# A layout edit: constants, dump and statistics move between activations and weight buffers, and two side chunks swap buffers

## What is computed

```
for i in range(DEPTH):                       # DEPTH = 2
    hn = rms_norm(h, gains[0])
    mix = retention(hn, ...) if i % 2 == 0 else gated_deltanet(hn, ...)
    h = h + rms_norm(mix, gains[1])
    ff = sq_relu_mlp(rms_norm(h, gains[2]), mlp_w_up[i], mlp_w_down[i])
    h = h + rms_norm(ff, gains[3])
```

## The kernel before

| | before |
|---|---|
| resid | 0 |
| act_hi, act_lo | 16, 32 |
| w_raw, w_hi, w_lo | 48, 64, 80 |
| gains | 96 |
| square (constants), dump, stat | 104, 105.5, 107.5 |
| big_at | 107.6875 |
| side_hi0 to 3; also hid_hi, y_hi, go_hi from the first | 107.6875 + 0, 8, 16, 24 |
| side_lo0 to 3; also hid_lo, y_lo, go_lo from the first | 107.6875 + 32, 40, 48, 56 |
| normed, raw_side, mix | 107.6875 + 64, 80, 80 |

## Time and profile before

### The profile page before, as it was taken

How to read it: one execution, slowest core, us unless ns; L and a number is a source line. 1 busy time by engine, 2 the same in 40 slices (tenths; PEclk the granted TensorE clock), 3 DMA queues, 4 the chain that set the end, 5 groups by cost and what they waited for, 6 DMA issues and landing times.

```text
span 1476.7 us, 19863 instructions
## 1 busy us (share of the span) xinstructions
PE 1448.8 (98%) x7772; PEld 1216.7 (82%) x7772; DVE 596.1 (40%) x1096; ACT 544.2 (37%) x1037; POOL 650.7 (44%) x303
## 2 busy tenths in 40 slices
PE   8999999999999999999999999999998999999998
PEld 7988888657889888888888977889988988888886
DVE  5551002363264420044037445797756640024224
ACT  5232233254253222223235457754734322123231
POOL 5244344443544443444546216357435444444442
PEclk9999999999999999999999999999999999999999
DMA  6222323400333223223232222221113132232321
GB/s 245 103 86 91 109 85 111 145 1 29 101 102 115 86 86 113 86 85 114 86 114 90 86 87 89 83 86 40 49 58 129 58 107 93 89 110 86 107 93 57
DMA packets 66557, 136.23 MB, mean 92 GB/s; under 512 B 3632, under 2 KB 4016, under 8 KB 66096
## 3 DMA queue, kind: packets, MB, share of 16 engines
q1 hardware_dynamic: 64016, 125.90, 25.9%
q10 hardware_dynamic: 2464, 9.25, 1.7%
HBM read 133.03 MB, written 2.11 MB: 92 GB/s over the span
## 4 chain that ended last, share of the span: by engine, by line
PE 89%; DVE 4%; ACT 2%; POOL 2%; DMA 1%; issue 1%; SPq 0%; DVEq 0%; ACTq 0%
PE bank L457 27%; PE bank L458 27%; PE bank L459 27%; PE bank L668 2%; POOL side_lo L332 1%; PE bank L782 1%; PE bank L654 1%; PE bank L738 1%; DVE mix L1614 1%; DMA w_raw<-in_ret_w_in_dram 1%; DVE gv L1846 1%; PE bank L505 1%; DVE act_lo L1656 0%; PE bank L686 0%; DVE resid L1612 0%
## 5 line engine op out<-in xcount | busy, mean ns | idle before, releaser
L332 POOL TENSOR_TENSOR w_lo<-w_raw,w_hi 128x1024 fp32r<-128x1024 f32 (+1 forms) x216 | 515.5, 2409 | 687.3 <-ACT w_hi L1058 675.5
L1058 ACT ACTIVATE w_hi<-w_raw 128x1024 fp32r<-128x1024 f32 x208 | 208.9, 1054 | 467.1 <-PE bank L459 424.5
L457 PE MATMUL bank<-act_hi,w_hi 128*128 128x512 f32 (+1 forms) x816 | 294.7, 361 | 6.6 <-DVE act_lo L1656 4.4
L459 PE MATMUL bank<-act_hi,w_lo 128*128 128x512 f32 (+1 forms) x816 | 293.0, 359 | 0.0
L458 PE MATMUL bank<-act_lo,w_hi 128*128 128x512 f32 (+1 forms) x816 | 292.9, 359 | 0.0
L458 PE MATMUL bank<-w_lo,hid_hi 128*128 128x512 f32 x480 | 189.0, 394 | 0.0
L457 PE MATMUL bank<-w_hi,hid_hi 128*128 128x512 f32 x480 | 188.3, 392 | 0.0
L459 PE MATMUL bank<-w_hi,hid_lo 128*128 128x512 f32 x480 | 186.5, 388 | 0.0
L1768 DVE TENSOR_TENSOR relu_sq<-relu 128x512 f32<-128x512 f32 x64 | 48.6, 759 | 328.6 <-ACT relu L1084 328.0
L457 PEld LDWEIGHTS bank<-act_hi,w_hi 128*128 128x128 f32 x816 | 154.7, 190 | 31.5 <-DVE act_lo L1656 5.5
L459 PEld LDWEIGHTS bank<-act_hi,w_lo 128*128 128x128 f32 x816 | 154.6, 189 | 22.7
(11 more groups left out here) (282 smaller groups left out, 2167.5 us busy)
## 6 DMA issues: line engine op xcount, KB each, us to landing
w_raw<-in_mlp_w_up_dram SPq DMA_DIRECT2D x32, 1024.0 KB, 5.7
w_raw<-in_mlp_w_down_dram SPq DMA_DIRECT2D x32, 1024.0 KB, 5.0
w_raw<-in_ret_w_in_dram SPq DMA_DIRECT2D x22, 1024.0 KB, 5.0
w_raw<-in_gdn_w_in_dram SPq DMA_DIRECT2D x16, 1024.0 KB, 5.4
w_raw<-in_ret_w_out_dram SPq DMA_DIRECT2D x8, 1024.0 KB, 4.9
w_raw<-in_gdn_w_out_dram SPq DMA_DIRECT2D x4, 1024.0 KB, 5.0
gains<-in_norm_gains_dram ACTq DMA_DIRECT2D x7, 512.0 KB, 6.2
raw_side<-in_ret_w_in_dram SPq DMA_DIRECT2D x2, 1024.0 KB, 15.0
```

The source lines that it names most:

```text
L332: done = nc.gpsimd.tensor_tensor(LO[slot][:, kt, :], RAW[raw][:, kt, :], HI[slot][:, kt, :].bitcast(F32), ALU.subtract)
L457: pe.matmul(dst, sta_hi, mov_hi, start=first, stop=False)
L459: return pe.matmul(dst, sta_lo, mov_hi, start=False, stop=last)
L1058: act.activation(HI[raw if slot is None else slot][:, kt, :], RAW[raw][:, kt, :], ACT.Copy)\
```

## The change

`square`, `dump` and `stat` (1536 + 2048 + 192 = 3776 bytes) are placed ahead of `w_raw` instead of behind `gains`. `w_raw`, `w_hi`, `w_lo` and `gains` thus lie 3.6875 KB higher: at 51.6875, 67.6875, 83.6875 and 99.6875; `square` is at 48. `resid`, `act_hi`, `act_lo` and everything from `big_at` on stay. In borders 0 and 3 chunk 2 takes slot 5 and chunk 3 slot 4, where it was the other way round. Nothing else differs.

```
@@ -85,16 +85,16 @@
     act_lo = plan.tile("act_lo", [P, KT, T], F32R, act_at + 16 * KB)
+    square = plan.tile("square", [P, 3, P], F32)
+    ident, tri, ones = (square[:, n, :] for n in range(3))
+    dump_at = plan.place(2 * KB)
+    dump = plan.tile("dump", [P, D], BF16, dump_at)
+    stat = plan.tile("stat", [P, 12, TT], F32)
     w_raw = plan.tile("w_raw", [P, 2, CK, GC], F32)
     w_hi = plan.tile("w_hi", [P, 2, CK, GC], F32R)
     w_lo = plan.tile("w_lo", [P, 2, CK, GC], F32R)
     gains_at = plan.place(8 * KB)
     gains = plan.tile("gains", [P, 2, D], F32, gains_at)
-    square = plan.tile("square", [P, 3, P], F32)
-    ident, tri, ones = (square[:, n, :] for n in range(3))
-    dump_at = plan.place(2 * KB)
-    dump = plan.tile("dump", [P, D], BF16, dump_at)
-    stat = plan.tile("stat", [P, 12, TT], F32)
@@ -136,7 +136,7 @@
-    HEAD_SLOTS = [(0, 1, 4, 5), (0, 1, 3, 4), (0, 1, 3, 4), (0, 1, 4, 5)]
+    HEAD_SLOTS = [(0, 1, 5, 4), (0, 1, 3, 4), (0, 1, 3, 4), (0, 1, 5, 4)]
```

## The result

The change makes the kernel slower: a median of 1483.58 us (1482.52 to 1484.27) against 1478.68 us before on the same chip, a ratio of 1.0031 with a 95% interval of 1.0020 to 1.0041. The forecast was 1466.2. The profiled execution has a span of 1482.5 us against 1476.7, so there are 5.8 us to find in the traces; the medians are 4.9 apart, since the profiled execution of the changed kernel is the longest of its seven.

The account below looks back on a forecast made before the run. The prediction took TensorE, busy 98% of the span, to bound the kernel. Its terms -4.3 - 3.9 + 0 - 2.5 - 0.8 - 0.4 = -11.9 us took 1478.1 to 1466.2 us, range 1450 to 1480.

Parts of the forecast that it names:

- The reading that distance sets the step: TensorE's time per matmul follows the distance from stationary to moving operand modulo 16 KB, 13.3 ns overhead at 0 or 8.
- the two classes modulo 16 KB: 256-column matmuls on side slots: 117.8 ns at distance 4.3125 KB (borders 0, 3), 113.33 at 12.3125 (borders 1, 2).
- Term (a): w against hid, y and go, 1,968 matmuls: 228.85 to 226.67 ns, -4.3 us.
- Term (b): Activations moving against w, 512 columns, 1,728 matmuls: 224.4 ns, -3.9 us, bounds -11.5 and +3.8.
- Term (c): Weights moving against activations, 512 columns, 960 matmuls: 0, bounds -6.4 and +2.1 us.
- Term (d): Activations against w, 256 columns, second token halves of four borders: 119.9 to 113.3 ns, -2.5 us; -0.8 at 117.8.
- term (e): Swapped side slots in borders 0 and 3: -0.8 us in second token halves, -0.4 in first halves.
- No cost for the other engines: POOL's subtraction, POOL, ACT and DVE, and DMA of weights: 0 us from the new places.
- The case in which gains and losses cancel: Rival: what hid stretches gain, activations against w lose; +0.8 us, 1478.9 us, chance 0.19.
- The slower case: Rival: 512-column streams of activations and w never settle, staying at 230 to 231 ns; about 1483 us, chance 0.15.
- Place costs nothing: Rival: the distances are a coincidence of stages, each term 0; 1478 us, chance 0.08.

Follow-up runs that it names:

- e1_place_alone: Small kernel of float32r matmuls on zeroed tiles, no other engine at work, stationary tile shifted in small steps: 226.7 ns at shift 0, 233.3 at 64.
- e4: Kernel before with only square and dump (3,584 bytes) moved ahead of w_raw, stat left behind: 1479.22 us against 1479.33, ratio 1.000.
- e7: Kernel before with 64 bytes behind stat, side tiles 1 and 2 moved 192 bytes, slots (0, 1, 3, 4) in all borders: 1475.56 us, ratio 0.9973.
- e8: Kernel before with only the swap of slots 4 and 5 in borders 0 and 3: 1479.42 us, ratio 0.9999.
- e2: Changed kernel with the old slots in borders 0 and 3, so the layout alone: 1484.3 us, ratio 1.0030 to before.
- e3: Kernel before with only the 192 bytes of stat moved ahead of w_raw: 1484.11 us, ratio 1.0031.
- e6_all_whole: Kernel before with a 64-byte gap behind stat, all matmul operands whole multiples of 256 bytes apart: 1477.21 us, ratio 0.9985.
- e10: Kernel before with 64 bytes behind stat, side tiles 1 and 2 moved 64 bytes, slots (0, 1, 3, 4) in all borders: 1474.17 us, ratio 0.9966.

## Why the prediction failed, point by point

**The reading that distance sets the step** was right in kind, and the key was wrong: it was taken modulo 16 KB, and it is modulo 256 bytes. The rows of before could not show it: every shift in them is 0 or 192 modulo 256, and each pair with 512 columns had one distance. The two 256-column steps, which are two steps of one shift, 113.33 and 117.8, happened to fall on the two classes modulo 16 KB twice each. The prediction saw the warning itself, in the earlier trace rows, where slot 3 had both steps, and went on with the classes.

**Term (a)** was exact: -4.3 us foreseen, -4.3 by the step and -4.2 by the stages.

**Term (b)**, activations moving over w, is the first step that failed: -3.9 us foreseen by carrying the gain of the 256-column form to 512 columns, +3.9 by the step of 228.9 (+3.5 by the stages). It is the bad end of its own bounds. The 256-column gain that it borrowed isn't one of place: the same addresses run at 113.3 and at 117.8.

**Term (c)**, w moving over activations, is the larger failure: 0 foreseen, bounds -6.4 and +2.1, and +6.4 measured. A shift and its mirror aren't alike (228.9 and 233.3), and no row of before had a mirrored shift, so the bound taken from the nearest rows was too narrow. By itself it is more than the whole net loss.

**Term (d)** came out at the lesser value that the prediction named, -0.8 in place of -2.5, and **term (e)** at 0 in place of -1.2, since the swap changes no shift modulo 256. Borders 1 and 2 lost 0.9 us that no term had. The misses add up: 7.8 for (b), 6.4 for (c), 1.7, 1.2 and 0.9 make 18.0, and -11.9 foreseen against +5.8 found is 17.7.

**No cost for the other engines** was right: POOL's subtraction into w and into side tiles takes the same time as in the earlier trace rows within 0.1 us, as its timeline shows (start, length), and TensorE stood idle for 27.4 us where it was 27.9.

```profile
1444.20 4.76 POOL L332 TENSOR_TENSOR w_lo<-w_raw,w_hi 128x1024 fp32r<-128x1024 f32 x2 [5.66 <-ACT w_hi L1058]
1448.92 4.73 POOL L332 TENSOR_TENSOR side_lo<-w_raw,side_hi 128x1024 fp32r<-128x1024 f32 x2
```

**The rivals.** The case in which gains and losses cancel had (a), (b), (d) and (e) as measured, and only (c) short: +2.1 for +6.4. The slower case had the time, 1483, by luck: nothing fails to settle at 230 to 231, the streams settle at 228.9 and 233.3, and (b) and (c) happen to average in between. It was priced at 0.15 and left out of the range, which ended at 1480. Its arithmetic held, since (3.9 + 6.4) / 2,688 = 3.8 ns is past the 3.0 from which it was to decide. "Place costs nothing", which the Trainium skill's "SBUF — State Buffer", section "SBUF: two separate sides", would give with TensorE's two independent read ports, is refuted by e1_place_alone: 226.7 or 233.3 ns with nothing else running.

**What stays open.** Why TensorE slows down at these shifts wasn't found; the runs show the rule, and that neither the own nor the next stationary tile decides alone. What makes a 256-column stream of float32r take 113.3 or 117.8 in a given place of the kernel stays open too, and with it why border 1 changed its step when only slots of other borders were swapped. The traces of the kernel give this much: behind w at a shift of 0, side slots at 192 ran at 113.3 in 8 of 16 second halves (before, e4, e7, e8); behind w at 192 they ran at 117.8 in all 12 (after, e2, e3).

## What to carry to other kernels

With float32r operands and 512 columns, put the tiles that meet in a matmul at whole multiples of 256 bytes from each other, and a tile of a few hundred bytes never between them without padding: one of 192 bytes cost this kernel 0.3%. With 256 columns a whole multiple is the slowest place instead (e6_all_whole), so give tiles of such stretches a shift of 64 or 192 (e7, e10). Measure the step as a stretch of unbroken matmuls divided by their number, since the durations of single matmuls (391 and 395 ns here) overlap and are no step. And before a difference between rows is made a rule, ask whether the same place also shows the other value; one such row was enough here to distrust it.

## What was not expected of the hardware

- The step of a float32r matmul depends on the shift of the stationary tile past the moving one modulo 256 bytes: 226.7, 233.3, 232.3 and 228.9 ns at 0, 64, 128 and 192 with 512 columns, up to 234.2 at 96. It isn't symmetric. bf16 (215.8) and float32 (two records of 429.2) don't show it, nor does float32r with 128 columns (111.7).
- With 256 columns shift 0 is the slowest, 120.0 ns, and the shifts 64 and 192 have two steady steps, 117.8 and 113.3, for the same addresses; at 192 it made the difference whether five or six matmuls at shift 0 ran ahead of the block.
